# The odd layer's stage ahead of a slot pair's products on TensorE, in a decoder step on one core

## The reference

```
for l in range(2):
    if l == 0: x += even_layer(x)     # convolution and gated linear attention
    else:      x += odd_layer(x)      # latent attention: z = norm(x) @ w_in; queries, keys and values
                                      # of 16 heads from a latent row; softmax; @ w_out
    x += peer(rms_norm(x))            # both groups of tokens
y = rms_norm(x)

def peer(h):                          # per token: 8 heads, 16 experts each
    q = (h @ w_q).reshape(n, 8, 2, 128)
    s = einsum('nhcd,hckd->nhck', q, sub_keys)     # two tables of 128 keys
    s_top, i_top = top_k(s, 16)                    # then the best 16 of the 256 sums
    ids = i1 * 128 + i2;  gates = softmax(c_top)
    act = gelu(einsum('td,thkd->thk', h, u_tab[ids])) * gates
    return einsum('thk,thkd->td', act, v_tab[ids])
```

## Time and profile before

| | |
|---|---|
| median of 3 executions | 3273.57 us (3271.82 to 3276.43) |
| profiled execution, its own time | 3271.82 us |
| span of its instructions | 3270.0 us |
| busy: TensorE matmuls, weight loads | 2424.8 us (74%), 1087.3 us (33%) |
| busy: VectorE, ScalarE, GpSimd | 2179.2 us (67%), 1561.9 us (48%), 1248.3 us (38%) |
| moved by DMA | 1240.64 MB, 379 GB/s over the span |
| of it by the gathers' queue | 1128.34 MB |
| mean granted TensorE clock | 0.848 of full speed |

### The profile page before, as it was taken

The page is one execution under the profiler, slowest core; times in us unless marked ns, Lnnn a source line. Parts: engine busy times, 40 slices in busy tenths (PEclk is TensorE's granted clock), DMA queues, the critical chain, the costliest instruction groups (busy, mean ns, idle before and its releaser), DMA issues. The chain is left out here.

```text
span 3270.0 us, 44315 instructions
## 1 busy us (share of the span) xinstructions
PE 2424.8 (74%) x15271; PEld 1087.3 (33%) x15271; DVE 2179.2 (67%) x5405; ACT 1561.9 (48%) x4415; POOL 1248.3 (38%) x1134
## 2 busy tenths in 40 slices
PE   8988777656678887676774688887767878676565
PEld 7644422111123443242232244432434434221121
DVE  4883566776676677755774566887666666676566
ACT  3112344434455556624553455666355655564344
POOL 0110343444443444434442444444344344443343
PEclk9979877767688899987897798999889889987587
DMA  4022899999999999999998999999999999999998
GB/s 174 1 86 80 364 426 426 426 427 427 427 421 376 421 422 422 424 388 413 426 426 327 379 411 417 422 421 423 375 426 426 426 425 426 426 424 425 425 416 355
DMA packets 215118, 1240.64 MB, mean 379 GB/s; under 512 B 27287, under 2 KB 62767, under 8 KB 72037
## 3 DMA queue, kind: packets, MB, share of 16 engines
q0 software_dynamic: 154368, 1128.34, 82.4%
q1 hardware_dynamic: 59229, 108.57, 8.8%
q10 hardware_dynamic: 1296, 0.90, 0.1%
HBM read 1233.74 MB, written 4.46 MB: 379 GB/s over the span
## 5 line engine op out<-in xcount | busy, mean ns | idle before, releaser
L1193 POOL DMA_INDIRECT p_rows<-in_peer_uv,p_ids x1024 | 1157.3, 1130 | 1668.2 <-PE p_acc L1819 1531.2
L1819 PE MATMUL p_acc<-p_rows,p_diag 64*64 64x512 f32 x8192 | 1284.3, 733 | 660.8 <-ACT p_diag L1324 640.4
L1595 DVE CUSTOM_DVE_ANT_0 p_rows<-p_rows,p_x_n 128x1024 f32<-128x1024 f32 x1040 | 1257.5, 1222 | 731.4 <-DMA p_rows<-in_peer_uv,p_ids 699.5
L1318 ACT ACTIVATE p_acts<-p_dots 128x1 f32<-128x1 f32 x1040 | 209.6, 202 | 1155.0 <-DVE p_dots L1595 1151.0
L1819 PEld LDWEIGHTS p_acc<-p_rows,p_diag 64*64 64x64 f32 x8192 | 272.5, 151 | 1410.1 <-ACT p_diag L1324 1228.2
L1324 ACT ACTIVATE p_diag<-p_unit,p_gated 128x64 f32<-128x64 f32 x1024 | 356.0, 348 | 33.4
L1320 ACT ACTIVATE p_gated<-p_acts,p_gates 128x1 f32<-128x1 f32 x1024 | 301.7, 295 | 33.2
L1751 PE MATMUL p_q_banks<-p_xT,p_w_q 128*128 128x256 f32 (+3 forms) x1088 | 242.8, 384 | 43.5 <-DMA p_keys<-in_keysT 40.0
L1751 PEld LDWEIGHTS p_q_banks<-p_xT,p_w_q 128*128 128x128 f32 x1088 | 205.2, 201 | 82.3 <-issue 54.3
L1318 ACT ACT_TABLE_LOAD x134 | 171.9, 1283 | 27.3 <-DVE p_dots L1595 25.0
L541 DVE SCALAR_TENSOR_TENSOR a_conv<-a_u,a_conv_wc,a_conv 128x512 f32<-128x512 f32 x120 | 86.6, 793 | 0.0
(11 more groups left out here) (421 smaller groups left out, 2665.8 us busy)
## 6 DMA issues: line engine op xcount, KB each, us to landing
p_w_q<-in_w_q_heads SPq DMA_DIRECT2D x35, 1024.0 KB, 10.1
p_rows<-in_peer_uv,p_ids POOLq DMA_INDIRECT x1024, 15.3
r_arena<-in_c_w_out SPq DMA_DIRECT2D x8, 1024.0 KB, 37.7
a_w_in<-in_ab_w_in SPq DMA_DIRECT2D x6, 1024.0 KB, 10.5
r_arena<-in_w_qx SPq DMA_DIRECT2D x16, 384.0 KB
r_arena<-in_c_w_in SPq DMA_DIRECT2D x2, 2688.0 KB, 12.0
r_arena<-in_w_q_heads SPq DMA_DIRECT2D x5, 1024.0 KB, 24.0
p_keys<-in_keysT SPq DMA_DIRECT2D x35, 128.0 KB, 12.5
```

What stands on the lines that cost most here:

```text
L1193: nc.gpsimd.indirect_dma_start(out=rows[:, slot % RING, :], out_offset=None, in_=w[f"peer_uv{of}"], in_offset=bass.IndirectOffsetOnAxis(ap ...
L1318: nc.scalar.activation(acts[:, i % 4, j:j + 1], dots[:, i % 4, j:j + 1], ACT.Gelu).then_inc(gelud, 1)
L1595: nc.vector.tensor_tensor_reduce(rows[:, k % RING, 0:D_MODEL], rows[:, k % RING, 0:D_MODEL], x, 1.0, 0.0, ALU.mult, ALU.add, dots[:, slot ...
L1819: last = nc.tensor.matmul(acc[64 * c:64 * c + 64, 512 * r:512 * r + 512], diag[of, slot // GROUP % 4, j, :], rows[of, (slot + j) % RING, a ...
```

## The change

On TensorE, the call that takes the next odd-layer stage moves from the end of the loop over groups to its start. It keeps its condition, its place relative to the head's queries (behind them), and its number: the k-th hooked group still takes stage k. No other engine's code changes.

```diff
                 if head is not None:
                     queries(head, "both")
                 for g in range(GROUPS):
+                    if hooked(n, g):
+                        next(steps, None)
                     experts(first_slot(n) + GROUP * g, ENDS.index(t), n % H_P == 0 and g == 0, n % H_P == H_P - 1 and g == GROUPS - 1)
                     if g == 1 and head is not None:
                         scores(m)
@@
                     if (n, g) == SPREAD_PE[1]:
                         smp_spread_x(1)
-                    if hooked(n, g):
-                        next(steps, None)
             if SMP_AT == NW:
                 sample_slots()
             for _ in steps:
```

## The result

The changed kernel takes **3301.01 us** in the median of five runs (3292.97 to 3307.21), the kernel before beside it 3274.86 us (3271.82 to 3276.43): a ratio of 1.008, with a 95% interval of 1.006 to 1.010. That is 26 us slower, where 8.5 were forecast. The profiled execution took 3307.21 us (span 3305.4 us), so the two profiles lie 35 us apart, 9 more than the medians.

What follows compares the result with a forecast made beforehand. The prediction took the DMA, at its ceiling rate nearly everywhere, as the bound. Profiled 3271.8 + 6.4 (weight stalls) + 2.9 (layer 0's end) + 1 (behind queries) + 0 = 3282.1, forecast 3282 us, range 3268 to 3296.

Steps and rivals of the forecast that it cites:

- The queue of 10 us: Gathers queued before the DMA engines: hides releases 2 to 6 us later, cost 0 unless something else has drained it.
- 9 of 10 nearly everywhere and the rate at 421 to 427 GB/s: Reading of the profile's DMA row and rate from slice 5 on, with few places where the DMA runs dry.
- The prediction's own signs of being wrong: DMA idle time in 940 to 2960 differing by under 2 or over 12 us, or median landings well below 12.
- Waits of the same group: TensorE's stages waiting for VectorE's or ScalarE's part of their group; releases 2 to 6 us later, hidden by the queue.
- E7 and H7 swap, their sum stays, and Q starts where it started: A head's last group: products (E) and stage (H) swap, queries (Q) start unmoved; taken as 0, bound 6.7 us gained.
- The queries' thin cover: Behind queries, nine of 24 heads have under 4 us above the least landing; +1 us, bounds 0 and 18.
- E0 with an empty H0: First group behind the queries in starving heads: its stage (H0) is empty, so its products (E0) don't move.
- The two stalls: Where project_out waits for output weights: products stand behind it, two gathers go out later; +3.2 us each, together +6.4.
- The end of layer 0: Last products start behind L2759 and total_sums, nothing hides it: +1.6 to +3.7 us, taken as +2.9.
- the last rival: Much slower, about 3296 us, chance 0.16: thin heads starve; longer merged waits would show as a lower mean granted clock.
- the much slower case: Late releases starve each of nine thin heads by 1.5 us, on top of the forecast: about 3296 us, chance 0.16.

Runs made afterwards that it cites:

- ring_7: Kernel before, each gather waiting for one more used slot while the stages run, so seven of eight buffers ahead: 3304.3 us, ratio 1.0092.
- after_split: Changed kernel with the next head's queries issued in halves, ahead of the first and second groups' products: 3293.5 us, ratio 1.0071 to the kernel before.
- all_ahead_split: Changed kernel with ScalarE's and VectorE's stages also moved ahead and the queries issued in halves: 3254.2 us, ratio 0.9944 to the kernel before.
- waits_only: Kernel before, with each stage's waits repeated ahead of the products and every matmul left in place: 3303.2 us, ratio 1.0090.
- last_only: Kernel before, with the stage moved ahead of the products only in each head's last group: 3286.3 us, ratio 1.0044.
- project_out_only: Kernel before, with only the first round's last eleven stages (output products and their weight waits) moved ahead, in either layer: 3279.6 us, ratio 1.0024.
- ring_6: Kernel before, each gather waiting for two more used slots while the stages run, so six of eight buffers ahead: 3369.0 us, ratio 1.0294.

## Why the prediction was wrong

The direction and the places it named were right, the size was not, and the step that failed is this: "The queue of 10 us hides that wherever nothing else has drained it: cost 0 there", together with the +1 us that it allowed behind the queries. The release does come later as said, by some 3 us. But the difference between median and least landing over a whole span is not a cover that every head has. The rule itself held in heads 22 to 24 of layer 0 and 22 to 27 of layer 1: releases 2.3 and 2.9 us later cost 0.3 us in each. In the three runs of heads with queries the change lost 13.9 us between the two profiles (5.7, 2.5 and 5.7), where the sum had 1, and in heads 6 to 11 of layer 1, without queries, 4.1, where it had 0. ring_7 takes 2.46 us of the supposed 10 and loses 30.7 us; with split queries it still loses 15.8, and after_split shows that the change loses as much with split queries as without. Nor was the cover nothing: at the prediction's own price for that case, 2 us in each of 368 groups, it would have been over 700 us.

That step rested on a reading that failed first: "9 of 10 nearly everywhere and the rate at 421 to 427 GB/s", with few windows in which the DMA runs dry. In the earlier trace rows slices 12 to 29 have 375 to 426 (and 327 at the layers' boundary), and only in slices 30 to 38 is it 424 to 426. The windows above say it without averages by eye: 409 GB/s at a share of 0.99 before, 425 at 1.01 later. By the packets in the trace the shares are 0.988 and 0.991 in the two stretches and 1.012 later, which is some 37 us of 1668 in which the DMA had less to do (an estimate). The gathers' packets take 280 ns in the mean in all three windows; what else the rate lacks goes with the other queues, which take 8 to 10% of the DMA's time in the two stretches and 2.5% later, and move fewer bytes in it (some 365 GB/s per unit of share against 418 for the gathers). Part of the 37 us could be won (all_ahead_split: 412 and 414), so the queue was already short too often in those heads, and lateness had something to cost.

The prediction's own signs of being wrong came true. The DMA's idle time from 940 to 2960, summed over windows of 5 us, is 42 us before and 57 after, 15 more, where it had set 12 as the most; 26 of these windows have a share under 0.9, where 15 had. And the landings in the median are at 11.8 and 10.8 us, under its 12.

Point by point:

- **Waits of the same group.** The prediction saw them ("many stages wait for VectorE's or ScalarE's part of the same group") and put them at zero on the strength of the cover. waits_only shows that they alone make the whole loss.
- **"E7 and H7 swap, their sum stays, and Q starts where it started"** held at the head it was read from (the last dot to the queries takes 7.9 us before and 7.6 after there) and in other heads not: 6.4 against 9.0 us at the head read above, 3.5 to 5.9 against 6.2 to 8.5 in heads 13 to 20 of layer 1. One head was taken for 22. last_only prices this step alone at 12.2 us.
- **The queries' thin cover, +1 with a bound of 18.** The count looked at the group behind the queries, and E0 with an empty H0 doesn't move against Q; but Q itself moved. The lateness entered one step earlier than the term looked.
- **The two stalls, +3.2 each.** The mechanism is as told: at the first, `project_out` starts at 1465.81, 27.4 us behind its head's first dot against 28.9 before, so the weights landed 1.5 us sooner (1.7 at most were allowed), and the windows behind it (below) show the DMA empty for a longer time, 7.5 us of idle time against 5.1 in windows of 2 us. project_out_only, at 2.9 us for each in the median, agrees with 3.2, though its profile doesn't show the place. In the changed kernel the first cost more (+7.4 us over three heads), the second +2.5 over two heads.
- **The end of layer 0, +2.9.** The last products stood behind L2759, as told, but ran at the upper clock level, so the last step came 1.6 us later after L2759 (7.23 us against 5.67 in the earlier trace rows), the lower bound of the term (the rows stand below).
- **The clock.** The mean granted clock fell from 0.848 to 0.835 in the profiled executions, as the last rival asked. But other executions of the kernel before have 0.834 to 0.848, those of the changed kernel 0.832 to 0.841, and waits_only has the whole loss at 0.848 to 0.852. A lower clock is not what made the loss. The products took less, not more, of the stretch (324.47 us for 2312 against 336.85 for 2304). Ahead of the queries, as in last_only above, the merged wait can put three steps in a row at the lower level.
- **The rivals.** 3301 is nearest to the much slower case, 3296, which asked for lateness above 2.6 us in each of nine thin heads. The lateness was there, and its 14 us behind queries are close to the 13.9 above, but that is in part luck: after_split loses as much without the long piece that was to starve those heads.

The first stall after, with the windows behind it, to set beside the earlier trace rows:

```profile
1465.81 6.52 PE L2409 MATMUL r_bank<-r_arena 128*128 128x256 f32 x16 [5.90 <-DMA r_arena<-in_c_w_out]
1472.26 1.95 PE L1819 MATMUL p_acc<-p_rows,p_diag 64*64 64x512 f32 x16
...
1473.65 1.08 POOL L1193 DMA_INDIRECT p_rows<-in_peer_uv,p_ids  x1 [11.97 <-PE p_acc L1819]
```

```profile
1465.00:1470.00 5.00, 4.19 (x10) 3.38 (x11) 0.00 (x0) 0.00 (x0) 0.00 (x0) 0.50 0.61 250
1470.00:1475.00 5.00, 5.00 (x28) 2.84 (x27) 2.63 (x6) 0.85 (x3) 1.08 (x1) 0.85 0.00 0
```

The end of layer 0 after, to set beside the earlier trace rows:

```profile
1773.16 0.16 DVE L2759 TENSOR_TENSOR s_share<-s_share,s_total 128x1 f32<-128x1 f32 x1 [2.63 <-ACT s_share L2653]
...
1780.39 0.22 DVE L2775 COPY smp_olT<-r_bank 128x32 f32<-128x32 f32 x1 [1.12 <-PE r_bank L2950]
```

The weights' landing moved by 1.5 us for two gathers less, 4.9 us of transfer. The Trainium skill, "DMA: Bandwidth & Descriptors", section "Issuing engines are not separate DMA queues", says that transfers started by different engines run on the same 16 DMA engines and interleave; the trace agrees in kind, since the weights came sooner with two gathers left out, but by a third of the gathers' time and not by all of it. Where the rest of that time went is not shown.

## What to carry to other kernels

When one engine's step is moved in a schedule written out by hand, look at what feeds it. If the inputs come from other engines' steps of the same turn, the move turns a finished input into one that has just been begun, and everything behind it in that queue waits too; move the steps on all engines together, or none. Measure the cover before relying on it, by a ring that is one buffer shorter, and read the result stretch by stretch: here two buffers less cost nothing in some heads and four fifths of 95 us in others. Neither the distance between median and least latency over the whole span nor a busy share of 0.99 had shown that.

## What the runs showed of the hardware

The DMA's busy share and its rate part ways: 0.99 goes with 409 GB/s in the two stretches and 1.01 with 425 later. The gathers' packets take the same 280 ns there and here; the difference lies in the share itself and in the other queues' transfers. With two gathers fewer out the rate falls faster than the share (ring_6: 0.95 and 384, which is 404 per unit of share against 413 before), and the gathers' packets take 285 ns in the mean. A kernel whose DMA was busy for 99% of those stretches was still made 0.56% faster as a whole, without a byte less to move.

The mean granted clock of one execution says little about a change: the same kernel had 0.834 to 0.848 in executions whose times lie within 0.4%, and the kernel with the added waits had the highest, 0.852, while it was 0.9% slower.
